# First norm of a hybrid encoder step: the token scale moved from the rows into the matrix that turns them

## The reference

```python
def rmsnorm(x, w):
    xf = x.astype(jnp.float32)
    y = xf * lax.rsqrt(jnp.mean(xf * xf, axis=-1, keepdims=True) + EPS)
    return (y * w.astype(jnp.float32)).astype(x.dtype)

def trunk_layer(x, dn_conv_buf, dn_state, sc_conv_buf, mem_k, mem_v, p):
    xn = rmsnorm(x, p['norm1_w'])
    proj = xn @ p['w_in']          # q, k, v, decay and gate logits, short conv, memory query, 3 gates
    ...                            # conv + gated delta rule, short conv, memory attention, merged by gates
    h = x + (merged @ p['w_o']).astype(x.dtype)
    h = h + moe(rmsnorm(h, p['norm2_w']), ...)   # top 4 of 32 experts
    return h, ...
```

## Time and profile before

| | us |
|---|---|
| median of 3 runs | 1408.0 (1406.7 to 1408.87) |
| the profiled execution | 1406.6 |
| its span | 1404.8 |
| PE busy | 1339.1 (95% of the span) |
| DVE busy | 460.0 (33%) |
| ACT busy | 233.5 (17%) |
| the chain that ended last | PE 73%, DMA 22%, DVE 3%, ACT 1% |

### The profile page before, as it was taken

How to read it: one execution, slowest core, us unless ns; L and a number is a source line. 1 busy time by engine, 2 the same in 40 slices (tenths; PEclk the granted TensorE clock), 3 DMA queues, 4 the chain that set the end, 5 groups by cost and what they waited for, 6 DMA issues and landing times.

```text
span 1404.8 us, 16557 instructions
## 1 busy us (share of the span) xinstructions
PE 1339.1 (95%) x7269; PEld 670.2 (48%) x7269; DVE 460.0 (33%) x864; ACT 233.5 (17%) x470; POOL 0.2 (0%) x4
## 2 busy tenths in 40 slices
PE   7999999999999999999999998899999999999996
PEld 4556677655554543443444434344343443434432
DVE  3465254263112432233232222323223222132233
ACT  4344231230001210110111101011010110101112
POOL 0000000000000000000000000000000000000000
PEclk9999999999999999999999999999999999999998
DMA  9443331011826799999999999999999999999994
GB/s 335 133 134 126 120 70 62 1 61 60 305 66 251 301 428 432 432 429 431 429 430 432 432 432 430 430 431 430 431 430 431 432 431 430 428 431 431 427 426 182
DMA packets 59547, 455.21 MB, mean 324 GB/s; under 512 B 14932, under 2 KB 26361, under 8 KB 44368
## 3 DMA queue, kind: packets, MB, share of 16 engines
q1 hardware_dynamic: 59328, 454.05, 78.5%
q10 hardware_dynamic: 144, 0.07, 0.0%
HBM read 449.46 MB, written 4.64 MB: 323 GB/s over the span
## 4 chain that ended last, share of the span: by engine, by line
PE 73%; DMA 22%; DVE 3%; ACT 1%; issue 0%; ACTq 0%; SPq 0%; DVEq 0%
PE ps L1150 32%; DMA sb_ring<-in_w_up_dram 20%; PE ps L809 9%; PE ps L616 9%; PE ps L1126 5%; PE ps L823 3%; PE ps L1035 3%; PE ps L589 3%; DMA sb_ring<-in_w_down_dram 2%; PE ps L1188 1%; PE ps L658 1%; DVE sb_xg L2126 1%; DVE sb_h L2197 1%; PE ps L904 1%; PE ps L1211 1%; PE ps L914 0%
## 5 line engine op out<-in xcount | busy, mean ns | idle before, releaser
L1150 PE MATMUL ps<-sb_ring,sb_xg 128*64 128x512 f32 x2048 | 457.6, 600 | 29.6 <-DMA sb_ring<-in_w_up_dram 24.2
L1150 PEld LDWEIGHTS ps<-sb_ring,sb_xg 128*64 128x64 f32 x2048 | 142.4, 138 | 298.8 <-issue 259.2
L1150 PE MATMUL ps<-sb_ring,sb_hidT 128*64 128x512 f32 x992 | 218.9, 594 | 2.3 <-DMA sb_ring<-in_w_down_dram 2.3
L1150 PEld LDWEIGHTS ps<-sb_ring,sb_hidT 128*64 128x64 f32 x992 | 72.5, 137 | 135.1 <-issue 134.4
L809 PE MATMUL ps<-sb_xn,sb_ring 128*128 128x384 f32 x384 | 132.6, 491 | 0.0
L616 PE MATMUL ps<-sb_xn,sb_ring 128*128 128x384 f32 x384 | 126.3, 487 | 1.3 <-DVE sb_xn L1747 1.3
L2159 DVE TENSOR_TENSOR sb_hg<-ps,sb_biases 128x512 f32<-128x512 f32 x32 | 22.1, 691 | 287.8 <-PE ps L589 287.8
L616 PEld LDWEIGHTS ps<-sb_xn,sb_ring 128*128 128x128 f32 x384 | 72.2, 190 | 50.4 <-DVE sb_xn L1747 1.4
L809 PEld LDWEIGHTS ps<-sb_xn,sb_ring 128*128 128x128 f32 x384 | 71.1, 190 | 48.8 <-issue 3.6
L2197 DVE TENSOR_TENSOR sb_h<-sb_h,ps 128x512 f32<-128x512 f32 x90 | 56.6, 683 | 103.4 <-PE ps L1188 103.2
L1126 PEld LDWEIGHTS ps<-sb_onehot,sb_xn 128*128 128x128 f32 x720 | 81.5, 192 | 12.2 <-issue 12.2
(11 more groups left out here) (325 smaller groups left out, 1047.8 us busy)
## 6 DMA issues: line engine op xcount, KB each, us to landing
sb_ring<-in_w_down_dram SPq DMA_DIRECT2D x26, 4096.0 KB, 28.0
sb_ring<-in_w_up_dram SPq DMA_DIRECT2D x26, 4096.0 KB, 30.7
sb_ring<-in_w_gate_dram SPq DMA_DIRECT2D x25, 4096.0 KB, 31.7
sb_ring<-in_w_gate_dram SPq DMA_DIRECT2D x14, 2048.0 KB, 15.9
sb_ring<-in_w_in_dram SPq DMA_DIRECT2D x11, 2048.0 KB, 10.0
sb_ring<-in_w_up_dram SPq DMA_DIRECT2D x11, 2048.0 KB, 16.0
sb_ring<-in_w_down_dram SPq DMA_DIRECT2D x9, 2048.0 KB, 29.6
sb_ring<-in_w_down_dram SPq DMA_DIRECT2D x6, 1024.0 KB, 21.9
```

Source lines behind the costliest of these rows:

```text
L1150: last = mm(o, x(k), columns(kind, w, i, j), start=(k == 0), stop=(k == KT8 - 1))
```

## The change

Tiles 0 to 2 are no longer scaled as rows. DVE multiplies the 128x128 identity by the token scales instead (`token_scales[t]`, a diagonal matrix, kept in the first 128 columns of `xs[:, t, :]`), and PE turns the unscaled tile `h[:, t, :]` by a matmul against this diagonal, in place of a transpose against the identity. The two memory tiles keep the transpose. On ACT each root comes right behind its square. On DVE the wait for `cst` comes first, then for each tile mean, inverse, scale, with the weighting of the tile before behind it. PE starts the first column group after `xT` 3 and `xTa` 1, takes its eight channel blocks in the order 4, 5, 6, 7, 0, 1, 2, 3, and waits for `xTa` 3 ahead of block 0.

```diff
+        token_scales = [xs[:, t, 0:P] for t in range(3)]
...
             def tokens_turned(t):
                 pe.wait_ge(S["xs"], t + 1)
-                src = xs[:, t, :] if t < 3 else xs_mem[:, t - 3, :]
                 b = 2 * t if t < 3 else 4 + 2 * (t - 3)
                 for k in range(KT8):
-                    last = tr(bank(b + k // 4)[:, (k % 4) * P:(k % 4 + 1) * P], src[:, k::KT8])
+                    o = bank(b + k // 4)[:, (k % 4) * P:(k % 4 + 1) * P]
+                    if t < 3:
+                        last = mm(o, h[:, t, k::KT8], token_scales[t], start=True, stop=True)
+                    else:
+                        last = tr(o, xs_mem[:, t - 3, k::KT8])
...
-            def columns_of(q, n, c):
+            def columns_of(q, n, c, order=range(KT8)):
                 weights_in(n, c)
                 bank_free(q)
-                for t in range(KT8):
+                for t in order:
+                    if q == 0 and t == 0:
+                        pe.wait_ge(S["xTa"], 3)
...
             pe.wait_ge(S["xT"], 3)
-            pe.wait_ge(S["xTa"], 3)
-            for q in range(2):
-                columns_of(q, 0, q)
+            pe.wait_ge(S["xTa"], 1)
+            columns_of(0, 0, 0, order=(4, 5, 6, 7, 0, 1, 2, 3))
+            columns_of(1, 0, 1)
...
-            x_square(0)
-            x_square(1)
-            x_root(0)
-            x_root(1)
-            x_square(2)
-            x_root(2)
+            for t in range(TILES):
+                x_square(t)
+                x_root(t)
...
             def x_scaled(t):
-                src, dst = (h[:, t, :], xs[:, t, :]) if t < 3 else (mem[:, t - 3, :], xs_mem[:, t - 3, :])
+                src, dst = (ident, token_scales[t]) if t < 3 else (mem[:, t - 3, :], xs_mem[:, t - 3, :])
...
-            x_mean(0)
-            x_inverse(0)
-            x_mean(1)
-            x_scaled(0)
-            x_inverse(1)
-            x_scaled(1)
-            x_mean(2)
             dve.wait_ge(S["cst"], 32)
-            x_weighted(0)
-            x_inverse(2)
-            x_scaled(2)
-            x_weighted(1)
+            for t in range(TILES):
+                x_mean(t)
+                x_inverse(t)
+                x_scaled(t)
+                if t:
+                    x_weighted(t - 1)
             x_weighted(2)
```

More of the change, by code:

```diff
@@ L609, in bank_free @@
                     pe.wait_ge(S["pjev"], PJ_BEFORE[q])
-            def columns_of(q, n, c):
+            def columns_of(q, n, c, order=range(KT8)):
                 weights_in(n, c)
                 bank_free(q)
-                for t in range(KT8):
+                for t in order:
+                    if q == 0 and t == 0:
+                        pe.wait_ge(S["xTa"], 3)
                     last = mm(bank(pj_bank(q))[:, 0:TOK], piece(TRUNK_SLOT[n])[:, t, c * P:(c + 1) * P], xnT[:, t, :],
-                              start=(t == 0), stop=(t == KT8 - 1))
+                              start=(t == order[0]), stop=(t == order[-1]))
                 last.then_inc(S["pj"], 1)
```

## The result

| | before | after |
|---|---|---|
| median | 1408.0 us (1406.58 to 1408.87, 5 runs) | 1413.21 us (1412.75 to 1415.27, 5 runs) |
| ratio to before | | 1.0044, 95% interval 1.0033 to 1.0055 |
| the profiled execution | 1406.6 | 1413.21 |
| its span | 1404.8 | 1411.4 |
| first projection matmul starts | 14.46 | 21.43 |

The kernel became slower by some 6 us (4.6 to 7.7 by the interval; the two medians differ by 5.2). In the profiled executions the first projection matmul starts 6.97 us later, the first expert matmul 7.01 us later, and the end of the span comes 6.6 us later.

What follows compares the result with a forecast made beforehand. PE bounds the trunk, so only the first projection's start counts: PE's start +0.5, tile 0's doubled instructions +1.7, tile 2's chain +0.5, together +2.7 us, median 1408.0 to 1410.7. The range for 8 in 10 was 1408.0 to 1413.5.

Steps and rivals of the forecast that it cites:

- the bound and the passing on: Whole kernel: PE bounds the trunk without slack; a shift of the first projection matmul goes through one to one.
- the chain: Front: mean 0 at 7.95 behind cst, mean 2 at 13.33 behind weighting 0, projection released by DVE near 17.2.
- the 0.44 us read from ACT's late end: First projection's wait: ACT's copies end at 14.36 against DVE's 13.92; the split wait removes this 0.44 us.
- the plain 0.116 to 0.118: PE's turning: us per instruction of the diagonal matmul at the higher clock, 16 instructions a tile, 1.86 us.
- 17.16: Front of the kernel: forecast start of the first projection matmul, against 14.46 before.
- the +2.7 of the sum: First projection's start: PE's start +0.5, tile 0's doubled instructions +1.7, tile 2's chain and turning less savings +0.5.
- the late clock: PE between tiles 1 and 2: clock rises 3.5 us later; start 20.2, +5.7, 1413.7 us; chance 0.20 for +3.4 to +5.7.
- the 19 named as a sign of being wrong: Front: a first projection matmul starting beyond 19 us would show the forecast wrong.
- the 128x128 scaling: DVE: narrower scaling taken as 0.22 us, between 0.18 (32 columns) and 0.29 (256), against 0.75 for 128x1024.
- the rows' 2: PE's turning: transpose 0.112 us against 2 x 0.116 for a float32 matmul call, a factor of 2.
- The rival that a call costs four transposes: PE's turning: 0.45 us a call at higher clock, 0.85 at lower; start 22.4, +7.9, 1415.9 us; chance 0.03.

Runs made afterwards that it cites:

- e1: Kernel after, but the matmul that turns a tile reads 128 neighbouring channels of h as weights, not every eighth; 1.0019 of before.
- e8: Kernel before with split wait, blocks 4 to 7 first, scale 2 ahead of weighting 0, ten constant matmul calls ahead of the turning; 1.0015 of before.
- e3: Kernel before, only the transposes of tiles 0 to 2 replaced by matmuls of the scaled rows against the identity, stride 8 kept; 1.0051 of before.
- e9: Kernel before with split wait, blocks 4 to 7 first, scale 2 ahead of weighting 0, four constant matmul calls ahead of the turning; 0.9986 of before.
- e7: Kernel before with only the split wait and blocks 4 to 7 first; 1.0002 of before.
- e5: Kernel after with ten constant matmul calls on PE ahead of the turning; single time 1416.03 us.
- e10: Kernel after with four constant matmul calls on PE ahead of the turning; single time 1414.37 us.
- e8b: Kernel before with split wait, blocks 4 to 7 first, and on DVE inverse 2 and scale 2 ahead of weighting 0; single time 1409.0 us.
- e4: Kernel after with weights of tile 0 read at stride 8, tile 1 at stride 4, tile 2 at stride 2; single time 1412.76 us.

## Why the prediction was wrong

Right were the bound and the passing on. The start of the first projection is the one number that counts: +6.97 there, +7.01 at the experts, +6.6 at the end, and a time ratio worth 4.6 to 7.7. As far as the first expert matmul the shift passes one to one in every execution here, but for the clock dips named above and below. Behind it single executions scatter: against before, the experts took 3.0 us less in e1's profiled execution and 2.0 more in e8's. So the passing on to the end is shown by the ratios, not by one execution: after, e1, e3, e8 and e9 all have the shift of their start within the interval. Right was the chain: mean 0 at 7.87 behind the wait for `cst` (7.95 forecast), mean 2 at 13.73 behind weighting 0 (13.33), 16 records a tile, the projection released by DVE with no second stop. The split wait and the row order cost nothing; alone, in e7, they move the start by -0.48, near the 0.44 us read from ACT's late end.

The step that failed is this one: "A matmul over `h` read with a stride of 8 is not in the trace; the transposes read with that stride too, so I take the plain 0.116 to 0.118." It measured 0.24. The transposes' load at that stride was no bound for the load of another mode, and L1126, from which 0.116 came, loads its weights without a gap. I took the nearest row of the same mode and the nearest row of the same stride, and neither had both. By that the results of tile 0 came at 13.12 instead of 12.61, and those of tile 2 7.56 us later instead of 3.80: 0.5 + 3.8 = 4.3 us, all of the 21.43 - 17.16 = 4.27 by which the start was off. With the stride taken away, e1 starts at 17.14, the forecast's 17.16, and its ratio is worth the +2.7 of the sum. That the two agree to 0.02 is partly luck: in e1 PE began 0.12 earlier than forecast, the clock rose at 12.9 and not at 12.3, and an instruction at the higher level took 0.112 and not 0.117.

The trace before held a sign of this that I did not read: its own transposes load more slowly where there is a stride. Without one (`pg`), at a stride of 4 (`g_sb`), and at a stride of 8 in tile 2 of the norm:

```profile
L589 PEld LDWEIGHTS ps<-sb_cst,sb_pg x6: 138/142/143, 500.4 to 500.9; 128*128 128x128 f32 x6
L589 PEld LDWEIGHTS ps<-sb_cst,sb_g_sb x4: 196/210/219, 508.2 to 508.6; 128*128 128x128 f32 x4
...
L589 PEld LDWEIGHTS ps<-sb_cst,sb_rq x8: 187/192/205, 12.0 to 12.8; 128*128 128x128 f32 x8
```

The stride costs a transpose's load 0.05 to 0.07 us, but its spacing only goes from 0.109 to 0.112 or 0.120. It hid behind the spacing that I read.

I had no bound on this price from above, so the range rested on the clock for its upper end. The measured 1413.21 lies in it by the late clock's 1413.7, and that is luck. The clock did rise later than taken, at 13.84 and not at 12.3, but at 0.240 on either level that cost next to nothing: e5, at the higher level throughout, needs 11.52 us for its turning against 11.72. The start itself, 21.43, is beyond the 19 named as a sign of being wrong. Smaller: the 128x128 scaling took 0.29, not 0.22, the upper of its two bounds; PE began at 8.92 against 8.86.

The Trainium skill's factor of 4 for transpose mode ("TensorE: Matmul & The Clock Gate", section "Terms") was put aside for the rows' 2. Without a stride the runs stand by 2: a call takes 2 x 0.113 us in e1, a transpose 0.109. With stride 8 the ratio of a call is 2 x 0.240/0.112 = 4.3 at the higher level. The Trainium skill gives no condition of stride there, so I do not claim that it meant this. The rival that a call costs four transposes, to which I gave 0.03, thus came nearest in price at the higher level (0.45 against 0.48 us a call), though at the lower one it says 0.85, where 0.48 was measured.

## What to carry to other kernels

Before a transpose is replaced by a matmul, price the matmul by a row that has both its mode and its access pattern; if no row has both, the price is open upward, and the range must say so. Work that one engine saves (here 0.46 us of DVE a tile) is worth nothing when the engine on the path pays for it. Where rows of one trace differ in the access pattern alone, their loads show whether the pattern has a price. An idle engine ahead of the critical stretch can be given harmless work so that its clock is up when the stretch begins; here that, an earlier scale and the split wait were together worth 2.25 us (the split wait alone 0.48), while constant work that overran cost 2.1. The same four calls did not keep the clock up in e10.

## What the runs showed of the hardware

A float32 weight load of 128 columns outside transpose mode takes 0.192 to 0.197 us at the higher level when its elements lie 4 or 8 bytes apart, and 0.329 to 0.338 at 16 or 32 bytes. At 32 bytes the matmuls are 0.240 apart at either clock level (after, e5, e10); at 4 bytes 0.213 at the lower and 0.113 at the higher (e1). So the stride costs little at the lower level and doubles the price at the higher. A transpose's load takes 0.142 at 4 bytes, 0.210 at 16 and 0.192 at 32 at the higher level, with a spacing of 0.109, 0.120 and 0.112. Why the modes differ here was not tried.

The rise of the clock is not tied to PE's start by a fixed time. In executions where PE began between 8.4 and 8.9 the record's length changed at 11.6 us (before), 12.9 (e1), 13.8 (after) and 14.5 (e3), and in e8b not before the turning's end at 13.7. The clock column says 1.00 throughout these stretches, so there the level has to be read from the instructions. It can also fall again: in e10, where PE stood idle from 6.58 to 8.54 between the constant work and the turning, it fell at 11.0 in the middle of the turning, and there the column shows it (0.53).

Later the clock can fall too. In e3 and e10 the first column groups were granted 0.86, which cost 1.7 us in either. In e4 and e8b the stretch from 174 to 190 us, with many matmuls of 16 columns, was granted 0.79 where the kernel before has 1.00, and the first expert matmul came 3.3 us later than the front explains. e4's row:

```profile
174.00:190.00 16.00, 16.00 (x157) 10.65 (x156) 1.10 (x3) 1.90 (x3) 0.00 (x0) 0.79 0.02 6
```

These executions are no proof of what brings it about. A single time of this kernel can be off by some 3 us through it, and the start of the projection is the better measure.
